# Diffusion step with two attentions and experts: the end of the second attention is issued in another order

## The reference

```
h = rmsnorm(x) * (1 + scale) + shift
attn1 = differential attention, 4 heads     # two softmax maps per head
attn2 = latent attention, 4 heads           # low-rank q and kv, shared rotary key
x = x + gate * (concat(attn1, attn2) @ w_o)
h = rmsnorm(x) * (1 + scale_f) + shift_f
x = x + gate_f * (swiglu(h) if layer 0 else top-2-of-8 experts(h))
```

## Time and profile before

| what | value |
|---|---|
| median of 3 runs | 2054.04 us (2053.56 to 2054.39) |
| the profiled execution's own time | 2051.91 us |
| its span in the profile | 2050.3 us |
| TensorE busy | 1996.1 us, 97% of the span |
| VectorE busy | 1528.1 us, 75% |
| ScalarE busy | 1140.7 us, 56% |
| granted TensorE clock, mean | 0.996 |
| end of the second attention, layer 0 and layer 1 | about 306 us and 1106 us from the start |

### The profile page before, as it was taken

How to read it: one execution, slowest core, us unless ns; L and a number is a source line. 1 busy time by engine, 2 the same in 40 slices (tenths; PEclk the granted TensorE clock), 3 DMA queues, 4 the chain that set the end, 5 groups by cost and what they waited for, 6 DMA issues and landing times. The chain is left out here.

```text
span 2050.3 us, 31301 instructions
## 1 busy us (share of the span) xinstructions
PE 1996.1 (97%) x11814; PEld 1775.3 (87%) x11814; DVE 1528.1 (75%) x1709; ACT 1140.7 (56%) x1389; POOL 239.2 (12%) x258
## 2 busy tenths in 40 slices
PE   8999999999999999999999989999999999999997
PEld 4898679999999999989878978888888888888884
DVE  5547676877767775755852479988899988989997
ACT  5217663322212223623864368777778878788774
POOL 1130100000000000121100037000000000100012
PEclk9999999999999999999999999999999999999999
DMA  9220432344453443321000089999999999999995
GB/s 340 77 90 6 146 113 93 114 164 149 134 169 134 155 132 96 125 69 67 1 1 22 7 325 385 386 386 386 386 386 386 386 386 387 386 387 386 386 387 203
DMA packets 267136, 447.17 MB, mean 218 GB/s; under 512 B 12993, under 2 KB 159393, under 8 KB 266881
## 3 DMA queue, kind: packets, MB, share of 16 engines
q1 hardware_dynamic: 246048, 375.74, 51.7%
q0 software_dynamic: 19120, 67.84, 9.1%
q10 hardware_dynamic: 1872, 2.26, 0.3%
HBM read 430.29 MB, written 16.63 MB: 218 GB/s over the span
## 5 line engine op out<-in xcount | busy, mean ns | idle before, releaser
L2013 DVE TENSOR_TENSOR w_lo<-mraw,w_hi 128x1792 fp32r<-128x1792 f32 (+2 forms) x306 | 643.3, 2113 | 89.0 <-ACT w_hi L1334 86.4
L1334 ACT ACTIVATE w_hi<-mraw 128x1792 fp32r<-128x1792 f32 (+2 forms) x306 | 541.6, 1775 | 174.0 <-PE ps L2710 156.7
L2708 PE MATMUL ps<-w_hi,xs_lo 128*128 128x448 f32 (+1 forms) x816 | 310.0, 380 | 4.8 <-DVE w_lo L2013 3.6
L2710 PE MATMUL ps<-w_hi,xs_hi 128*128 128x448 f32 (+1 forms) x816 | 305.0, 374 | 0.0
L2709 PE MATMUL ps<-w_lo,xs_hi 128*128 128x448 f32 (+1 forms) x816 | 304.7, 373 | 0.0
L1456 DVE TENSOR_TENSOR sub_lo<-zone,sub_hi 128x1024 fp32r<-128x1024 f32 (+2 forms) x112 | 128.3, 1147 | 152.0 <-ACT sub_hi L1005 151.8
L2708 PEld LDWEIGHTS ps<-w_hi,xs_lo 128*128 128x128 f32 x816 | 153.3, 188 | 30.2 <-DVE w_lo L2013 11.2
L2710 PEld LDWEIGHTS ps<-w_hi,xs_hi 128*128 128x128 f32 x816 | 153.2, 188 | 19.2
L2709 PEld LDWEIGHTS ps<-w_lo,xs_hi 128*128 128x128 f32 x816 | 153.4, 188 | 17.8
L2284 PE MATMUL ps<-f_hi,sub_lo 128*128 128x320 f32 x704 | 162.2, 312 | 0.7 <-DVE sub_lo L1456 0.7
L2284 PE MATMUL ps<-f_hi,sub_hi 128*128 128x320 f32 x704 | 161.5, 310 | 0.0
(11 more groups left out here) (368 smaller groups left out, 3667.8 us busy)
## 6 DMA issues: line engine op xcount, KB each, us to landing
mraw<-in_moe_w_down SPq DMA_DIRECT2D x68, 1024.0 KB, 14.5
mraw<-in_moe_w_gate SPq DMA_DIRECT2D x68, 896.0 KB, 13.0
mraw<-in_moe_w_up SPq DMA_DIRECT2D x68, 896.0 KB, 13.1
in_cos<-in_w_mods POOLq DMA_DIRECT2D x72, 512.0 KB, 3.7
mraw<-in_moe_w_gate SPq DMA_DIRECT2D x34, 1024.0 KB
mraw<-in_moe_w_up SPq DMA_DIRECT2D x34, 1024.0 KB
mraw<-in_moe_w_down SPq DMA_DIRECT2D x34, 768.0 KB, 14.7
zone<-in_w_in SPq DMA_DIRECT2D x13, 1024.0 KB, 5.2
```

The costliest lines, as they stand in the source:

```text
L1334: nc.scalar.activation(w_hi[:, n % SPLITS, a], mraw[:, n % MRING, a], ACT.Copy).then_inc(w_hi_ready, 1)
L2013: nc.vector.tensor_tensor(w_lo[:, n % SPLITS, a], mraw[:, n % MRING, a], w_hi[:, n % SPLITS, a].bitcast(f32), ALU.subtract).then_inc(w_spl ...
L2708: nc.tensor.matmul(out, a_lo, b_hi, start=start, stop=False)
L2710: return nc.tensor.matmul(out, a_hi, b_hi, start=False, stop=stop)
```

## The change

- `plan()`: the two shift-row products are gone; the output products now begin at the pair at column 1024 in both layers.
- Items: for the last item (16) of the second attention the transposes go to columns 0 to 767 and the values to 768 to 895, which are the score columns of even items. They no longer wait for the copy or the evacuation of other items, and are issued at the end of step 15, before the values of item 15. ACT copies both transposed blocks (15 and 16) in its step 15.
- The first output product is cut: chunk 0 is issued in step 14 ahead of the values of item 13, chunk 1 after the values of item 16, chunks 2 and 3 after the last `turn_out`, chunks 4 to 7 after the last `o_split`. `keep_busy` goes.
- The shift rows are written by SP to DRAM, element by element, right behind the gate rows, and read back as a broadcast to `shift_row` by two DMAs of 512 KB once the second attention of layer 1 is out. `add_shift` waits for these.

```diff
# plan()
-        if l:
-            for c in range(2):
-                m(("shift_row", c), "shift_row_ready", c + 1)
+        while len(main_freed) % 3 != 1:
+            left_out()
# placement
+        def turned_at(f, i=0):
+            return 3072 if f == 0 else 0 if i == N_ITEMS - 1 else 2048
+        def values_at(f, lat, i=0):
+            return turned_at(f, i) + 768 if lat else ADA_AT
# SP, behind the gate rows
+            for c in range(2):
+                sp.dma_start(shift_rows[c].rearrange("(k p) -> p k", p=P), mod[:, 1, 24:32, c], allow_slow_non_contiguous=True).then_inc(shift_rows_moved, 16)
+            sp.wait_ge(shift_rows_moved, 32)
+            sp.wait_ge(pv_evac, items_before(DEPTH, 0))
+            for c in range(2):
+                sp.dma_start(shift_row[c], shift_rows[c].partition_broadcast(P)).then_inc(shift_rows_moved, 16)
# ACT, attention
+                        if f and i == N_ITEMS - 1:
+                            values_out(i - 1)
+                            continue
                         act.wait_ge(tr_done, it + 1)
                         if i:
                             values_out(i - 1)
+                        turned(i)
+                        if f and i == N_ITEMS - 2:
+                            act.wait_ge(tr_done, it + 2)
+                            turned(i + 1)
# ACT, behind it
-                if l:
-                    for c in range(2):
-                        act.wait_ge(main_done, MAIN[("shift_row", c)] + 1)
-                        nc.scalar.activation(shift_row[c], ps[:, o:o + 1024], ACT.Copy).then_inc(shift_row_ready, 1)
# DVE, add_shift
-                dve.wait_ge(shift_row_ready, 2)
+                dve.wait_ge(shift_rows_moved, 64)
# TensorE, transposes(i) and values(i)
+                        last = f and i == N_ITEMS - 1
-                        if i:
+                        if i and not last:
                             pe.wait_ge(pt_ready, it)
-                        if i > 1:
+                        if i > 1 and not last:
                             pe.wait_ge(pv_evac, it - 1)
# (values: the pv_evac wait goes for the last item in the same way)
# TensorE, the loop over items
-                        transposes(i)
+                        if not f or i < N_ITEMS - 1:
+                            transposes(i)
                         beside(i)
+                        if f and i == N_ITEMS - 2:
+                            transposes(i + 1)
# TensorE, first(i)
+                    if i == N_ITEMS - 3:
+                        pe.wait_ge(exp_done, items_before(l, 1) + N_ITEMS - 1)
+                        claim_main(("o", l, 0))
+                        pe.wait_ge(o_split, N_TURN * l + TT)
+                        first_out(0, 1)
+
+                def first_out(k0, k1):
+                    return split_both(("o", l, 0), [p[:, k0:k1, :] for p in split_sub(("o", l, 0))], h_hi, h_lo, k0, k1, KC)
# TensorE, behind the attention
+                first_out(1, 2)
                 turn_out(1, M_TILES[-1], N_TURN - 1)
-                if l == 0:
-                    keep_busy(("o", l, 0), 2, x_t[:, 0, :])
-                else:
-                    for c in range(2):
-                        (eight matmuls for shift row c)
+                first_out(2, 4)
                 pe.wait_ge(o_split, N_TURN * (l + 1))
-                for d_ in range(KC):
+                first_out(4, KC).then_inc(main_done, products(("o", l, 0)))
+                for d_ in range(1, KC):
```

More of the change, by code:

```diff
@@ L376, in build @@
     gate_rows = nc.dram_tensor("gate_rows", (2, D_MODEL), f32).ap()
+    shift_rows = nc.dram_tensor("shift_rows", (2, D_MODEL), f32).ap()
     silu_rows = nc.dram_tensor("silu_rows", (2, P, KC), f32).ap()
@@ L627, in build @@
         no_tokens, tokens_out, tokens_in, rows_out = (sem(n) for n in ("no_tokens", "tokens_out", "tokens_in", "rows_out"))
-        shift_row_ready, xg_ready, router_ready = sem("shift_row_ready"), sem("xg_ready"), sem("router_ready")
+        shift_rows_moved = sem("shift_rows_moved")
+        xg_ready, router_ready = sem("xg_ready"), sem("router_ready")
         logits_out, onehot_ready, first_x = sem("logits_out"), sem("onehot_ready"), sem("first_x")
@@ L1160, in values_out @@
                         act.wait_ge(pv_done, it + 1)
-                        o = values_at(f, lat)
+                        o = values_at(f, lat, i)
                         if f == 0:
@@ L1184, in squares, with turned @@
                         ins.then_inc(head_sq, 1)
+                    def turned(i):
+                        nt, o = 6 if item(f, i)[2] else len(item(f, i)[1]), turned_at(f, i)
+                        nc.scalar.activation(pt_buf[:, i % 2, 0:nt, :], ps[:, o:o + nt * P].rearrange("p (k n) -> p k n", k=nt),
+                                             ACT.Copy).then_inc(pt_ready, 1)
                     exps(0)
@@ L1191, in attention @@
                             exps(i + 1)
-                        nt = 6 if item(f, i)[2] else len(item(f, i)[1])
+                        if f and i == N_ITEMS - 1:
+                            values_out(i - 1)
+                            continue
                         act.wait_ge(tr_done, it + 1)
@@ L1195, in attention @@
                             values_out(i - 1)
-                        o = turned_at(f)
-                        nc.scalar.activation(pt_buf[:, i % 2, 0:nt, :], ps[:, o:o + nt * P].rearrange("p (k n) -> p k n", k=nt),
-                                             ACT.Copy).then_inc(pt_ready, 1)
+                        turned(i)
+                        if f and i == N_ITEMS - 2:
+                            act.wait_ge(tr_done, it + 2)
+                            turned(i + 1)
                         if f == 0 and i:
@@ L1952, in flat @@
                 return a.rearrange("p t e o -> p t (e o)")
-            shift_rows = [shift_row[t // (TT - 1)] for t in range(TT)]
+            shift_of = [shift_row[t // (TT - 1)] for t in range(TT)]
             def add_shift(t):
                 dve.wait_ge(htok_scaled, t + 1)
-                dve.wait_ge(shift_row_ready, 2)
-                nc.vector.tensor_tensor(htok[:, t, :], htok[:, t, :], shift_rows[t], ALU.add).then_inc(htok_ready, 1)
+                dve.wait_ge(shift_rows_moved, 64)
+                nc.vector.tensor_tensor(htok[:, t, :], htok[:, t, :], shift_of[t], ALU.add).then_inc(htok_ready, 1)
             link(nc.vector.tensor_tensor(cmp_a[:], by_o, by_e, ALU.is_gt))
@@ L2432, in transposes @@
                             pe.wait_ge(vm_ready, 2 * l + 1)
-                        o = turned_at(f)
+                        o = turned_at(f, i)
                         for k in range(6 if item(f, i)[2] else len(item(f, i)[1])):
@@ L2442, in values @@
                         pe.wait_ge(pt_ready, it + 1)
-                        if i:
+                        if i and not (f and i == N_ITEMS - 1):
                             pe.wait_ge(pv_evac, it)
-                        o = values_at(f, lat)
+                        o = values_at(f, lat, i)
                         if lat:
@@ L2580, in beside @@
                         turn_out(*turn_at(i), turns_before(i))
+                    if i == N_ITEMS - 3:
[5 more added lines that the diff above has]
+                    return split_both(("o", l, 0), [p[:, k0:k1, :] for p in split_sub(("o", l, 0))], h_hi, h_lo, k0, k1, KC)
                 attention(1, last_value_rows, lambda: pe.wait_ge(vm_early, 2 * l + 2), beside, first)
+                first_out(1, 2)
                 turn_out(1, M_TILES[-1], N_TURN - 1)
-                pe.wait_ge(exp_done, items_before(l + 1, 0))
-                pe.wait_ge(pv_evac, items_before(l + 1, 0))
-                if l == 0:
-                    keep_busy(("o", l, 0), 2, x_t[:, 0, :])
-                else:
-                    pe.wait_ge(mod_rows, 2 * len(MODS))
-                    for c in range(2):
[L2594 to L2599, removed]
+                first_out(2, 4)
                 pe.wait_ge(o_split, N_TURN * (l + 1))
-                for d_ in range(KC):
+                first_out(4, KC).then_inc(main_done, products(("o", l, 0)))
+                for d_ in range(1, KC):
                     claim_main(("o", l, d_))
```

5 lines of the change are left out of this document (removed).

## The result

The changed kernel takes 2039.79 us, median of 4 runs (2039.62 to 2040.80); the kernel before, run beside it, 2054.03 (2053.56 to 2054.39). The ratio is 0.9932, 95% interval 0.9915 to 0.9949: faster by 14.2 us, 0.7%. I had forecast 2048.8, a gain of 5.2, and a range from 2046.5 to 2052.1. The direction was right, the size was not.

The account below looks back on a forecast made before the run. The order of waits bound the attention, TensorE layer 1 from its first output product, DMA the expert stage. 1.90 + 3.78 - 0.5 = 5.2 us off the median 2054.04 gave 2048.8 us, range 2046.5 to 2052.1.

Parts of the forecast that it names:

- Part 1: In step 14, chunk 0 ahead of item 13's values waits for DVE's low part, making the chain 3.25 us late.
- the clock: Half clock after TensorE's new 2.32 us idle time in step 14: nothing to 1.6 us per layer, 0.5 charged in all.
- the first rival: Half clock follows the new TensorE idle time in step 14: 2049.9 to 2051.5 us, chance 0.18.
- Part 2: End of the second attention: early transposes and copy of item 16 win back 1.98 of 3.25 us lost.
- Part 3: Chunks 1 to 7 around the last turn: product 0 ends 1.90 us earlier in layer 0, 3.78 in layer 1.
- Part 4: Shift-row copies and DMAs cost nothing: writes land by 1115, broadcasts by 1129, with some 43 us to cover them.
- Does it carry: Behind the first residuals, later stages move along, so both layers' gains count in full: 5.7 us.
- Half clock behind the new gap: TensorE runs at half clock after its new idle time in step 14: 2049.9 to 2051.5 us, chance 0.18.
- Step 14 cost nothing instead of more: Rival: step 14 costs more than it brings, chain 2 to 3 us late, some 2051 us; chance 0.12.
- The shift rows were not late: Rival: shift rows reach `add_shift` too late, slower by over 0.2% if they land after 1182.3; chance 0.03.
- the order did take effect: Rival: early transposes still wait for item 15; only the shift rows' 1.88 us and some chunks won; chance 0.03.
- the low end of the range: Whole kernel at 2046.5 us: half a us more for each layer, no clock loss and 0.8 of scatter.

Follow-up runs that it names:

- experiment 1: The changed kernel with chunk 0 moved ahead of the values of item 13: 2047.64 us, ratio 0.9979 to the kernel before.
- experiment 3: The changed kernel with the last item back in the shared columns and ordinary order: 2041.94 us, ratio 0.9959 to the kernel before.
- experiment 6: The kernel before with only the shift rows moved to DMA: 2052.52 us, again 2052.50; with two unused matmuls filling the wait in both layers 2049.29.

## Why the prediction was right or wrong

**The step that failed is Part 1**, "chunk 0 in step 14", with its "3.25 us late ... it is the price of the change, and nothing hides it". I took the added lines for a part of `first(i)`, which runs ahead of `values(i - 1)`. They stand at the end of `beside(i)`, which runs behind `transposes(i)`. The lines of context above them (the late columns and `turn_out`) are those of `beside`, so the code said it, and the change section above repeats the mistake. Put in its true place chunk 0 hardly waits (1090.56, with DVE's part done at 1090.41) and lies in the idle 1.16 us. My sum had 3.25 us of delay in each layer where the trace shows none. With my own other terms it becomes 1.90 + 3.25 = 5.15 in layer 0 and 3.78 + 3.25 = 7.03 in layer 1, 12.2 us. The trace has 5.42 and 7.31. Of the 9.0 us between forecast and result 6.5 are this step, 0.5 the clock, 0.5 small sizes (below) and 1.5 the median that I started from.

That the arithmetic was sound shows in experiment 1, where the lines are where I had them: 2.27 for my 2.32 us of idle time, 3.24 for 3.25 late, 2.18 us gained in layer 0 for 1.90, and by the medians 3.7 us in all for 5.2 (4.7 by the local intervals). There the first rival came true in one layer.

**Part 2, the last item ahead: right.** 1.98 forecast, 2.1 measured in experiment 3.

**Part 3, chunks under waits: right.** The turn starts 7.09 us after the values of item 14 (1091.57 to 1098.66); my working has 7.2 (1100.6 to 1107.80). It delays the product by 0.36 us, not 0.46, and the six chunks behind it take 5.28, not 5.36 (1099.02 to 1104.70 less the 0.40 between the end of a product and its residual, 7.54 less 7.14). These three, 0.28 us together, account for the 0.27 us by which each layer beats the corrected sum.

**Part 4: right, one term mis-sized.** The pair of 4 KB writes took 15.5 us for my 12.3, one broadcast pair 5.5, and nothing waited. The 1.88 us of the rows I had counted as a term of their own. Chunks 2 and 3 fill the hole that the rows leave, and without them the term is not safe: in experiment 6 one execution lost 1.6 of it to half clock, and the medians with the hole empty show no gain.

**Does it carry: yes.** From the first residual of layer 1 to the first add it took 60.44 us before (1117.80 to 1178.24) and 60.44 after (1104.70 to 1165.14). Only the end gave something back in this execution: from the first residual of layer 1 to the end of the span it took 934.5 us and before 932.5. The clock is 0.66 and 0.65 in the two stretches from 2003 to 2013; the two at the same place before (2013 to 2023) have 0.95 and 0.71. That is about 7 us at half clock against 3.4, an estimated 1.7 of the 2.0 us, and most of why the two spans differ by 11.1 us and not by 12.7.

**The clock: wrong for this change, right as a mechanism.** I charged 0.5 us for a wait that does not exist. Half clock did come behind waits of 1.57, 1.80 and 2.27 us, but each of them also stood in an execution or a layer with a clock of 1.00 behind it, and the 1.16 us of every round showed it in none of the profiled executions. The Trainium skill (TensorE: Matmul & The Clock Gate, Part 1) holds that half speed is the default and activity releases it. The trace agrees at 0.62 and 0.52 behind the 2.27 us of experiment 1, layer 1, and does not behind the 2.27 us of the same kernel's layer 0.

**The rivals.** Half clock behind the new gap had no gap to stand behind. Step 14 cost nothing instead of more. The shift rows were not late and the order did take effect. None of the rivals lay on the side of a larger gain, and the low end of the range allowed half a us for each layer: both only varied the size of steps that I took as read.

**The median.** From it the sum of 12.7 us would have given 2041.3, 1.5 above the result, for the first runs of the kernel before lay in the upper half of its scatter.

## What to carry to other kernels

Before an added piece is priced, find the function that encloses it and the call order around it: the same six matmuls cost 3.24 us of delay ahead of a wait for DVE and nothing 2 us later, in an idle gap of the round. In a chain of waits, put independent work exactly into the gaps, cut to their size. When work is taken off TensorE, fill the hole it leaves in the same way or expect that the gain may go to the clock. Judge differences below 0.2% by an interval of the trace that holds just the edit, and against runs of the same mean clock.

## What the hardware showed that I had not expected

The same program at the same idle time runs on at full clock in one execution and at half clock in another (0.70 and 0.50 against 1.00 and 1.00 in layer 0, behind 1.8 us). Runs of the kernel before differ by up to 6.3 us (2048.67 to 2054.93), and the mean is 2052.66 at a mean clock of 0.995 and 2050.29 at 0.996, so a good part of this goes with the clock. And of two like pairs of 4 KB writes in single elements the second took longer: 12.4 us for the gate rows, 15.5 for the shift rows issued 1.9 us behind them. That the first pair still in flight is the reason is my guess; no run separates it.
